# Streaming encoder layer with top-k attention: the searches of tiles 6 to 9 moved into the first block, split between ScalarE and VectorE

## What is computed

```
dots  = einsum('bqhd,bkd->bqhk', qi, ki)                  # 8 index heads of 32
score = einsum('bqh,bqhk->bqk', wi, relu(dots)) * INDEX_SCALE
score = where(key_chunk <= query_chunk, score, -inf)      # chunks of 64
_, sel = top_k(score, min(256, Lk // 4))
logits = einsum('bqgrd,bqkgd->bqgrk', q, k[sel]) * ATTN_SCALE + bias
o = softmax(logits) @ v[sel]
```

## Time and profile before

| | us |
|---|---|
| median of three runs | 1968.95 (1968.7 to 1971.7) |
| the profiled execution | 1971.94 |
| its span, first instruction to last | 1970.1 |
| first block, to the first instruction of the second | 916 |
| second block | 1054 |

### The profile page before, as it was taken

One profiled execution on the slowest core, in us unless ns is written; L12 is line 12 of the kernel. 1 busy time (PEld: TensorE's weight loads), 2 busy tenths in 40 slices (PEclk: granted clock), 3 DMA queues, 4 the chain that ended last, 5 costly groups with the idle time before them and its releaser, 6 DMA issues.

```text
span 1970.1 us, 17750 instructions
## 1 busy us (share of the span) xinstructions
PE 1664.9 (85%) x5151; PEld 877.9 (45%) x5199; DVE 1324.7 (67%) x3127; ACT 841.2 (43%) x1553; POOL 437.5 (22%) x336
## 2 busy tenths in 40 slices
PE   3999899879996999582788888878888888889997
PEld 2555455445554555271334434434443434444543
DVE  4232756677777556613346999989999999988322
ACT  2121323323333343312147777756756756442332
POOL 0000101100001000001234443433333322334333
PEclk9999899989997999695789888989999999999999
DMA  7440210111110011104521211101210101101001
GB/s 302 54 74 27 67 42 32 54 60 38 48 37 31 35 37 38 56 19 122 172 74 43 91 58 59 38 31 54 63 38 27 41 15 43 38 6 43 18 15 37
DMA packets 82706, 107.39 MB, mean 55 GB/s; under 512 B 15429, under 2 KB 61061, under 8 KB 82354
## 3 DMA queue, kind: packets, MB, share of 16 engines
q1 hardware_dynamic: 81578, 102.59, 15.7%
q10 hardware_dynamic: 1032, 3.67, 1.7%
HBM read 67.15 MB, written 39.09 MB: 54 GB/s over the span
## 4 chain that ended last, share of the span: by engine, by line
DVE 23%; PE 20%; issue 6%; another core or an unknown queue 1%; ACT 1%; POOL 1%; SPq 1%; DMA 0%; POOLq 0%; DVEq 0%; ACTq 0%
DVE above L307 8%; PE wide L1485 6%; PE wide L1500 5%; DVE max_junk L1564 4%; PE bank L1455 2%; PE bank L1468 2%; PE bank L1470 2%; PE bank L1469 2%; DVE S L341 1%; PE bank L1473 1%; DVE den L1579 1%; DVE reach L345 1%; DVE shift L1574 1%; DVE above L342 1%
## 5 line engine op out<-in xcount | busy, mean ns | idle before, releaser
L761 PE MATMUL bank<-hT,W 128*128 128x512 f32 (+1 forms) x1280 | 497.6, 534 | 2.1 <-DVE gst L986 2.1
L1349 POOL TENSOR_TENSOR E<-E,EB 128x512 f32<-128x512 f32 x174 | 255.7, 1473 | 523.4 <-ACT E L1430 523.3
L1430 ACT ACTIVATE E<-bank 128x512 f32<-128x512 f32 x290 | 172.1, 594 | 403.1 <-PE bank L1473 329.3
L1455 PE MATMUL bank<-k,qh 128*128 128x512 f32 (+3 forms) x320 | 206.4, 667 | 135.8 <-DVE mxp L1564 106.3
L761 PEld LDWEIGHTS bank<-hT,W 128*128 128x128 f32 x1280 | 219.5, 192 | 194.3 <-issue 186.0
L1564 DVE CUSTOM_DVE_ANT_0 max_junk<-bank,mask 128x512 bf16<-128x512 f32 (+3 forms) x344 | 199.6, 601 | 155.2 <-PE bank L1455 117.9
L1485 PE MATMUL wide<-E,vx 128*128 128x512 f32 x544 | 289.1, 614 | 13.2 <-POOL E L1349 10.4
L307 DVE TENSOR_SCALAR_CACHE_REDUCE above<-S,search 128x1152 bf16<-128x1152 f32 (+9 forms) x143 | 244.7, 1711 | 0.8
L1034 DVE SCALAR_TENSOR_TENSOR S<-relu,wi,S 128x1024 f32<-128x1024 f32 (+7 forms) x182 | 169.4, 959 | 88.9 <-ACT relu L741 88.0
L741 ACT ACTIVATE relu<-wide 128x1024 f32<-128x1024 f32 (+7 forms) x208 | 155.2, 765 | 167.6 <-PE wide L776 130.1
L1396 ACT ACTIVATE act_junk<-S,minus_cand 128x1152 bf16<-128x1152 f32 (+9 forms) x132 | 197.0, 1492 | 1.7
(11 more groups left out here) (169 smaller groups left out, 2022.7 us busy)
## 6 DMA issues: line engine op xcount, KB each, us to landing
q<-q_scratch SPq DMA_DIRECT2D x68, 128.0 KB, 2.9
xs<-x_prompt SPq DMA_DIRECT2D x16, 512.0 KB, 4.2
xr<-x_prompt SPq DMA_DIRECT2D x16, 512.0 KB, 5.1
y_prompt<-osb SPq DMA_DIRECT2D x16, 512.0 KB, 3.7
W<-w_in SPq DMA_DIRECT2D x8, 768.0 KB, 17.6
gb<-gb_scratch SPq DMA_DIRECT2D x17, 256.0 KB, 5.3
ma<-ma_scratch SPq DMA_DIRECT2D x17, 256.0 KB, 4.7
W<-w_in SPq DMA_DIRECT2D x8, 532.0 KB, 8.9
```

The costliest lines, as they stand in the source:

```text
L761: mm = pe.matmul(out, stationary(c), moving(c), start=(c == 0), stop=(c == DC - 1))
L1349: pool.tensor_tensor(E[:, k % 4], E[:, k % 4], EB[:, kv * GRP:(kv + 1) * GRP, off:off + P], ALU.mult)\
L1430: act.activation(E[:, k % 4], banks[2 + k % 2][:].rearrange("p (j n) -> p j n", j=GRP), ACT.Exp).then_inc(fl_free, 1)
L1455: pe.matmul(banks[k % 2][:, 0:b - a], qh[:, t % 2, kv, j, :], keys[:, a:b], start=True, stop=True)\
```

## The change

EARLY is now tiles 2 to 9, and FIRST is 10. In the first block the searches are split as in the second: ScalarE normalises (AN) and does rounds 0 to 12 (AK), VectorE takes over minus_cand and does rounds 13 to 25 (SR) and the choice (SM). Se has two slots. A planner in phase1_steps, searches, deals rounds to each tile's run of steps until about 20 us of estimated cost, and in_order spreads them over it one by one. A tile's search begins at the earliest two tiles later, and when the mask of two tiles before has been planned. Scores are spread over all five contractions of a tile instead of two, all heads of the first chunk before those of the second; S holds two chunks in place of two rows, each chunk is reduced and stored by itself, and the scores of tiles 0 and 1 are dropped.

In the second block one tile's rounds are spread over 26 attention jobs, counted through all steps (PACE): ScalarE's for tiles 10, 11, ... begin at jobs 0, 26, ..., VectorE's and the choice 26 jobs later. Maxima lie from 0.12 to 0.82 of a step. VectorE multiplies the mask in place, SyncE stores it in mask_scratch and loads it again with the others.

```diff
-EARLY = range(TOPK // P, 6)
-SEARCH_PIECES = [(0, 3), (3, 7), (7, 10), (10, 13), (13, 16), (16, 20), (20, 23), (23, 26)]
+EARLY = range(TOPK // P, 10)
...
+def round_cost(t):
+    return key_tiles(t) * P / 960 + 0.6
...
+    act_todo = [(t, r) for t in EARLY for r in range(-1, ZOOM_AT)]
+    dve_todo = [(t, r) for t in EARLY for r in range(ZOOM_AT, ALL_ROUNDS + 1)]
+    masked = {EARLY[0] - 2, EARLY[0] - 1}
+
+    def searches(tile_time, budget):
+
+        acts, dves = [], []
+        cost = 0
+        behind = act_todo[0][0] if act_todo else NT
+        while dve_todo and cost < budget and dve_todo[0][0] < behind:
+            v, r = dve_todo.pop(0)
+            dves.append(("SR", v, r) if r < ALL_ROUNDS else ("SM", v))
+            cost += round_cost(v) * (1 if r < ALL_ROUNDS else 6)
+        cost, first = 0, []
+        while act_todo and cost < budget:
+            u, r = act_todo[0]
+            if r == -1 and (tile_time < u + 2 or u - 2 not in masked):
+                break
+            act_todo.pop(0)
+            if r == -1:
+                first.append(("SL", u))
+            acts.append(("AN", u) if r == -1 else ("AK", u, r))
+            cost += round_cost(u)
...
-            k = -(-len(pending) // 2)
-            project(("TM", t), k)
+            left = 5 if nt == 4 else 17
+            project(("TM", t), left)
...
+            first, acts, dves = searches(t, 20.0 if nt == 4 else 1000.0)
+            segment = steps[begin:]
+            del steps[begin:]
+            steps += first + in_order((segment, 0.0, 1.0), (acts, 0.02, 0.98), (dves, 0.02, 0.98))
+            if t >= TOPK // P:
+                pending += [("I", t, h, c) for c in range(len(score_chunks(t))) for h in range(NIH)]
...
-        S = sb(st, "S", [P, 2, SEQ], F32)
+        S = sb(st, "S", [P, 2, 1024], F32)
...
+        Se = sb(st, "Se", [P, 2, key_tiles(EARLY[-1]) * P], F32)
...
+                        for i in range(2):
+                            sp.wait_ge(s_out[i], stores_of(i, chunks_to(t)))
+                        if t == EARLY[0] + 1:
+                            sp.wait_ge(bias_out, 16)
+                        if t >= EARLY[0] + 2:
+                            sp.wait_ge(m_ready, t - EARLY[0] - 1)
+                        sp.dma_start(Se[:, t % 2, 0:n], s_dram[t, :, 0:n]).then_inc(Se_in[t % 2], 16)
...
+                    elif s[0] == "AN":
+                        u = s[1]
+                        act.wait_ge(enough_set, NT - EARLY[0])
+                        act.wait_ge(Se_in[u % 2], 16 * ((u - EARLY[0]) // 2 + 1))
+                        act_normalise(act, halved, Se[:, u % 2, 0:key_tiles(u) * P], unit[:, u:u + 1])
...
+    PACE = 26
...
+    begins = [2 * sum(key_tiles(u) for u in range(t)) for t in range(NT + 1)]
+
+    def in_step(t, items, first, last):
+
+        if not 0 <= t < NT:
+            return []
+        every = [(first + (last - first) * i / len(items), x) for i, x in enumerate(items)]
+        a, b = begins[t], begins[t + 1]
+        return [([x], (g - a) / (b - a), (g - a) / (b - a)) for g, x in every if a <= g < b]
...
     def dve_step(t):
-        u = t + 2
-        rounds = [("R", u, r) for r in range(ZOOM_AT, ALL_ROUNDS)] if searched(u) else []
-        return in_order((rounds, 0.0, 0.8), ([("M", *m) for m in maxima_of(t + 1)], 0.08, 0.78),
+        rounds = []
+        for u in range(FIRST, NT):
+            items = [("R", u, r) for r in range(ZOOM_AT, ALL_ROUNDS)] + [("C", u)]
+            rounds += in_step(t, items, PACE * (u - FIRST + 1), PACE * (u - FIRST + 2))
+        return in_order(*rounds, ([("M", *m) for m in maxima_of(t + 1)], 0.12, 0.82),
...
-                        ([("C", u)] if searched(u) else [], 0.9, 0.9))
...
+                    for u in range(FIRST, NT):
+                        if mask_step(u) == t - 1:
+                            sp.wait_ge(m_ready, u - FIRST + 1)
+                            n = key_tiles(u) * P
+                            sp.dma_start(m_dram[u, :, 0:n], B.reach[:, 0:n]).then_inc(m_out, 16)
+                            load_S(u + 3)
+                    load_mask(t + 2)
```

334 lines of the change are left out of this document (165 added, 169 removed).

## The result

| | before | after |
|---|---|---|
| median of four runs, same chip, us | 1970.08 (1968.7 to 1971.7) | 2012.57 (2010.82 to 2018.97) |
| the profiled execution | 1971.94 | 2010.82 |
| its span | 1970.1 | 2009.0 |
| first block | 916 | 1009.5 |
| second block | 1054 | 999.5 |

The changed kernel is slower: ratio 1.0215, 95% interval 1.020 to 1.0229. The forecast was 1939. The second block won 55 us (forecast: 60), the first lost 93 (forecast: 30).

What follows compares the result with a forecast made beforehand. VectorE was taken to bound stretches 4 to 13 of the second block, TensorE the first block. -60 us there and +30 in the first made -30: 1942 us for the profiled execution, 1939 for the median, range 1882 to 1985.

Steps and rivals of the forecast that it cites:

- Second block: Attention block: search moved out of VectorE-bound stretches gains 72 us, less two losses of 6 each: 60 us less, bounds 30 and 90.
- the early stretches: Second block, from tile 4: the larger engine's need plus up to 8 us; tiles 4 and 5 at 41 and 44.
- two things are given back: Second block: choices among maxima make TensorE wait, 6 us; ScalarE's early normalising, load and rounds in steps 0 to 3, 6.
- rival B: Second block: rounds inside the maxima and choices starve TensorE, cutting the gain from 60 to 30 us: 1969 us; chance 0.13.
- no engine is full in the sum, so the cost lies where a stage has none to spare: First block: added VectorE and ScalarE search costs only where a stage is full; sum +30 us, bounds 0 and 85.
- Tile by tile: First block stretches: tile 13 +5, tile 9 +4, tiles 5 and 6 +3 each, tile 8 -4 us.
- gst term: First block: TensorE's k/q transposes wait 12 times for VectorE's gst; a round in front adds 0.5 a time: +6 us.
- Block heads: First block: ScalarE's rounds and normalising enter the serial transposes and copies: +3 before tile 4, +8 before tile 8, -4 for tile 12.
- rival C: First block: ScalarE's normalising waits for store, load and mask, holding bank copies; block pays 85 us: 1994 us; chance 0.17.
- Last block: End of first block: tile 9's rounds and choice +11 us, full score chunks in a row -5 or -6: +6 us.
- The clock: Second block: a steadier feed would return part of the clock, granted at 0.93 in stretch 9 and 1.00 in stretch 14.
- rival A: Both blocks: the whole gain, 85 us in the second and nothing lost in the first, 1884 us; chance 0.18.

Runs made afterwards that it cites:

- f5: Changed kernel with each tile's scores put back half in the next tile's TM contraction, the rest in its Q, searches left alone: 1979.01 us.
- h2: Changed kernel with the edits of f4 and f5 together: 1976.01 us.
- f4: Changed kernel with the load of scores at 0.2 of a tile's run of steps, ScalarE's rounds from 0.35, VectorE's from 0.4: 1986.08 us.
- j2: h4 with tile 9's search back in the second block and ranges of jobs that differ from tile to tile: 1963.7 us.
- h4: Changed kernel with the edits of h1 and f5 together: 1973.39 us.
- f1: Changed kernel with the first block's search left out (no normalising, rounds or choices; masks zero): 1912.58 us.
- f2: Kernel before the change with the first block's search (tiles 2 to 5) left out in the same way as f1: 1945.06 us.
- e1: Changed kernel with ScalarE's normalising and first-block rounds placed from 0.30 of each tile's run of steps instead of 0.02: 2003.67 us.
- h1: Changed kernel with the load of scores, normalising and ScalarE's rounds behind the four H steps at block heads: 2004.35 us.
- j4: h1 with, in SyncE's list alone, the store of a mask due shortly before H steps moved behind the last of them: 2003.97 us.

## Why the prediction was wrong, point by point

**Second block, right, with some luck.** -54.7 us against -60, bounds 30 and 90. Only 46.7 of it came in stretches 4 to 15, which were to give all; the other 8 us came in the first four stretches and behind the last nmax, which the working left as they were. VectorE's busy time there is 674.6 us, forecast 675. The forecast of the early stretches held: tiles 4 and 5 at 42.3 and 41.5 (41, 44). Tiles 6 to 10 came 5 to 9 us longer each than forecast and tile 11's 10 shorter. The term "two things are given back" was too small for choices among maxima: over the stretches of tiles 5 to 13 TensorE still waited 71.8 us for mxp, forecast under 50 after 88.9, once for 10.9 us at a stretch, the length of a choice:

```profile
PE bank L1532 <- DVE mxp L1636: 71.8, 37, 10.9
```

So rival B's mechanism was there, at some 13 us in place of its 30. Stretch 12 stayed at 85, stretch 13 came to 79 (76).

**First block, wrong: the step "no engine is full in the sum, so the cost lies where a stage has none to spare".** It made each stretch the larger of two engines' work plus a little, and so priced 63 us more on VectorE (its own terms give 65) and 187 on ScalarE at 30 us. The work was over-sized: measured were 54 and 159 us more. The price was too low: the search as a whole cost 0.22 us per us before and 0.29 after, the added part 0.33 (69.3 us for 213), and against the same kernel without search every stretch from tile 3 on was longer, by 1 to 18 us. The rest of the 93 us is 24.3 that no search is needed for. Tile by tile: tile 13 +8.6 (forecast +5), tile 9 +5.4 (+4), tile 5 +8.4 and tile 6 +10.6 (+3 each), tile 12 +10.3 (nothing), tile 8 -0.8 (-4), tile 11 -2.3 (-4).

**The gst term was mis-sized.** +6 us, 0.5 a time: it counted the round in front of gst. Measured are 38.5 us, 3.0 a time, since what stands in front of gst is a backlog on VectorE of up to two rounds and two scores, not one round. ScalarE's rounds have little part in it (54.6 with them thin, against 38.5 with VectorE's thin). f5 takes the scores away and leaves the rounds: 18.0.

**The scores' spread over all contractions had no price at all** in the working, where it is named only for the last block. Undoing it won 33.3 us (f5), and 4.6 where the rounds stood late (h2 after f4).

**Block heads.** +8 for tile 7's stretch, measured +21.5; +3 for tile 3's, measured +5.9. The prediction named the wait for the load of Se (41.4 us over seven waits, so about 6 each, in rival C's range), but not who else stands behind SyncE's stores: the loads of x. The rounds and the normalising in front of the hT copies, which the section on the change points at, were the small part: 12.9 of the 16.0 us at tile 8's head are there without them, behind the store of the scores.

**Last block.** +6; stretches 15 and 16 took 18.3 and 3.4 more. With tile 9's search out (j2 against h4) they came 8.3 and 8.2 us shorter; another part is there without any search (f1 against f2, 94.4 and 84.7 us for tile 15), and no run shows where these 10 us come from. The 5 us that full chunks in a row were to win are there: tile 16's stretch took 69.0 us in f1 and 74.1 in f2.

**Rival C** had the sign and nearly the first block's size (85 us), was 18 us short for the whole (1994), and its point of decision, 976 us, was passed. Its mechanism was only a part: with ScalarE's waits for Se gone (e1) 9 us came back, and with SyncE's order at the heads mended instead (h1, then j4) 9 us by the first nmax.

**The clock** was in the prediction as a possible gain (rival A). In the first block it was a loss: TensorE's 801.9 busy us at 0.89 against 777.2 at 0.93, with no term for it in the +30. Tile 7's stretch was granted 0.75 in the mean, which is half of it at 1.2 GHz and half at 2.4, and TensorE idled there for 31 of 82.7 us. The Trainium skill (Perfetto Trace Analysis, Optimization Strategy) says that interleaving regimes with different most-contended engines may improve performance, which is what this change does. The regimes were told apart rightly; that the borrowed engines' work would be free beside TensorE was not so here: +93 for -55.
